# A two-block transformer kernel: SBUF buffers allocated in another order

## What is computed

```
x = first_block(x, ...)    # mod = silu(c) @ w_ada; h = rms_norm(x) * (1 + sc1) + sh1
                           # h @ w_in -> HGRN2, dilated attention, conv module; gates = sigmoid(h @ w_gate)
                           # x += g1 * rms_norm(merged @ w_o)
                           # y = square(relu(h @ w_up)) @ w_down ; x += g2 * rms_norm(y)
return second_block(x, ...)  # the same frame: mLSTM and differential attention with a context of 256
                             # tokens, then (silu(gate) * val) @ w_down with a depthwise conv of 3
```

## Time and profile before

| | |
|---|---|
| median of 3 runs | 3175.56 us (3174.21 to 3181.29) |
| span of the profiled execution | 3166.6 us; its whole time was not recorded, so 9.0 us lie between its span and the median |
| granted TensorE clock, mean | 0.995 of 2.4 GHz |
| PE busy | 98% of the span, 23,974 matmuls |
| PEld busy | 93% |
| DVE, ACT busy | 75%, 42% |
| DMA | 722.62 MB, 228 GB/s over the span |

### The profile page before, as it was taken

How to read it: one execution, slowest core, us unless ns; L and a number is a source line. 1 busy time by engine, 2 the same in 40 slices (tenths; PEclk the granted TensorE clock), 3 DMA queues, 4 the chain that set the end, 5 groups by cost and what they waited for, 6 DMA issues and landing times.

```text
span 3166.6 us, 55394 instructions
## 1 busy us (share of the span) xinstructions
PE 3099.8 (98%) x23974; PEld 2933.4 (93%) x23974; DVE 2369.1 (75%) x2843; ACT 1334.2 (42%) x1459; POOL 1.8 (0%) x10
## 2 busy tenths in 40 slices
PE   7999999999999999999999999999999999999997
PEld 6899999999999999998988999989889989999996
DVE  4799876688887889899978765644767666767766
ACT  3343344444444443333463334422455444344444
POOL 0000000000000000000000000000000000000000
PEclk9999999999999999999999999999999999999999
DMA  9864444498894887777855763354343475655743
GB/s 395 333 216 168 162 158 149 173 352 344 328 366 160 311 306 273 269 264 288 297 186 212 274 256 139 134 217 160 120 147 134 174 265 187 226 213 201 258 177 136
DMA packets 106417, 722.62 MB, mean 228 GB/s; under 512 B 11677, under 2 KB 15389, under 8 KB 27197
## 3 DMA queue, kind: packets, MB, share of 16 engines
q1 hardware_dynamic: 100368, 703.64, 59.6%
q10 hardware_dynamic: 5806, 15.43, 1.6%
HBM read 712.41 MB, written 6.55 MB: 227 GB/s over the span
## 4 chain that ended last, share of the span: by engine, by line
PE 90%; DVE 6%; DMA 1%; ACT 1%; issue 1%; ACTq 0%; DVEq 0%
PE gemm L1040 40%; PE gemm L1049 19%; PE gemm L1076 12%; PE gemm L1079 6%; PE mix L1040 1%; DVE sb_parts L1781 1%; PE mix L1291 1%; PE mix L1571 1%; DMA sb_arena<-x_t 1%; ACT sb_parts L539 1%; DMA sb_raw<-stream 1%; DVE sb_arena L1836 1%; PE gemm L1207 1%; PE mix L1049 1%; PE mix L1150 1%
## 5 line engine op out<-in xcount | busy, mean ns | idle before, releaser
L539 ACT ACTIVATE sb_parts<-sb_raw 128x2048 fp32r<-128x2048 f32 (+2 forms) x489 | 899.6, 1842 | 1464.1 <-PE gemm L1049 958.9
L1781 DVE TENSOR_TENSOR sb_parts<-sb_raw,sb_parts 128x2048 fp32r<-128x2048 f32 (+2 forms) x489 | 1071.9, 2193 | 301.7 <-PE gemm L1049 149.9
L1040 PE MATMUL gemm<-op_h,sb_parts 128*128 128x256 f32 x7232 | 876.5, 278 | 1.1 <-ACT sb_parts L539 0.6
L1040 PEld LDWEIGHTS gemm<-op_h,sb_parts 128*128 128x128 f32 x7232 | 853.2, 188 | 2.5 <-ACT sb_parts L539 1.0
L1049 PE MATMUL gemm<-op_h,sb_parts 128*128 128x256 f32 x3616 | 455.4, 278 | 0.0
L1049 PEld LDWEIGHTS gemm<-op_h,sb_parts 128*128 128x128 f32 x3616 | 434.8, 188 | 0.2 <-DVE sb_parts L1781 0.2
L1076 PE MATMUL gemm<-op_up,sb_parts 128*128 128x512 f32 x1728 | 418.0, 392 | 3.0 <-DVE op_up L2410 3.0
L1076 PEld LDWEIGHTS gemm<-op_up,sb_parts 128*128 128x128 f32 x1728 | 315.3, 188 | 65.4 <-DVE op_up L2410 4.8
L1079 PEld LDWEIGHTS gemm<-op_up,sb_parts 128*128 128x128 f32 x1728 | 218.3, 188 | 10.5
L1762 DVE CUSTOM_DVE_ANT_0 sb_raw<-sb_raw,sb_arena,sb_vec 128x2048 f32<-128x2048 f32 x96 | 224.3, 2348 | 1.1
L1079 PE MATMUL gemm<-op_up,sb_parts 128*128 128x256 f32 x1728 | 220.6, 278 | 0.0
(11 more groups left out here) (360 smaller groups left out, 3340.3 us busy)
## 6 DMA issues: line engine op xcount, KB each, us to landing
sb_raw<-stream SPq DMA_DIRECT2D x597, 1024.0 KB, 5.0
sb_raw<-stream SPq DMA_DIRECT2D x64, 704.0 KB, 4.1
sb_arena<-stream SPq DMA_DIRECT2D x14, 1024.0 KB, 7.9
sb_arena<-stream SPq DMA_DIRECT2D x10, 768.0 KB, 8.2
sb_raw<-stream SPq DMA_DIRECT2D x6, 768.0 KB, 7.2
sb_arena<-c_rows ACTq DMA_DIRECT2D x3, 1024.0 KB, 8.4
bias_rows<-sb_arena ACTq DMA_DIRECT2D x1, 2304.0 KB
sb_arena<-x_t ACTq DMA_DIRECT2D x4, 512.0 KB, 19.1
```

The lines of the kernel that those rows point to most:

```text
L539: act.activation(parts[:, b % 2, 0, 0:kt, :], slot_of(slot)[:, 0:kt, :], ACT.Copy).then_inc(hi_ready, 1)
L1040: ins = pe.matmul(out, l, r, start=(opens and i == 0 and x is xh), stop=False, skip_group_check=True)
L1781: dve.tensor_tensor(parts[:, b % 2, 1, 0:kt, :], slot_of(slot)[:, 0:kt, :], parts[:, b % 2, 0, 0:kt, :].bitcast(F32), ALU.subtract).then_i ...
```

## The change

The order of the allocations. `small` (512 bytes) and `mod1` (384 bytes) come first and fill the space from byte 4,224 to 5,120. The arena follows at 5,120 (5 x 1,024), then `raw` at 153,600 (150 x 1,024), `parts` at 186,368 (182 x 1,024), `ident` at 219,136, `ones` at 219,648, and the rest behind them. Sizes, shapes and the use of every buffer stay as they were, and each engine's instructions are the same in the same order; only addresses in them differ.

```diff
-        raw = sb("raw", [P, SLOTS, KT, P])
-        parts = sb("parts", [P, 2, 2, KT, P], F32R)
-        ident = sb("ident", [P, P])
-        ones = sb("ones", [P, P])
-        vec = sb("vec", [P, NVEC])
-        sel = sb("sel", [P, 8])
-        head_sum = sb("head_sum", [P, 64])
+        small = sb("small", [P, 128])
         mod1 = sb("mod1", [P, 96])
-        mod2 = sb("mod2", [P, 2, 96])
-        lvl_mask = sb("lvl_mask", [P, 8, P], U8)
-        rstd = sb("rstd", [P, 512])
-        small = sb("small", [P, 128])
         ARENA = 37120
...
-        max_rows = rstd[0:8, :]
         opYd = operand("yd", 12288, 2, 8, S)
         opU2 = paired("up2", 12288, UP2)
         arena = sb("arena", [P, ARENA])
+        raw = sb("raw", [P, SLOTS, KT, P])
+        parts = sb("parts", [P, 2, 2, KT, P], F32R)
+        ident = sb("ident", [P, P])
+        ones = sb("ones", [P, P])
+        vec = sb("vec", [P, NVEC])
+        sel = sb("sel", [P, 8])
+        head_sum = sb("head_sum", [P, 64])
+        mod2 = sb("mod2", [P, 2, 96])
+        lvl_mask = sb("lvl_mask", [P, 8, P], U8)
+        rstd = sb("rstd", [P, 512])
+        max_rows = rstd[0:8, :]
```

## The result

The changed kernel takes 3238.43 us (median of 4 runs, 3238.04 to 3239.46), the kernel before 3178.26 us (4 runs, 3174.21 to 3181.29). The ratio is 1.0194 with a 95% interval of 1.0164 to 1.0223: slower by 60 us. The forecast was 3131 us, 1.4% faster, with a range of 3105 to 3217. The 60 us are some twice the distance between the shortest and the longest run of the kernel before that is on record (3166.67 to 3196.79 us).

A forecast was written before the change was run, and what follows sets the result against it. PE was taken to bound the kernel, busy for 98% of the span. Slow stretches -27.9, mixed stretches -12.9, down projections -3.8, other engines and DMA 0, sum -44.6 us: 3175.6 to 3131.0 us, range 3105 to 3217.

The forecast's parts named there:

- The two paces: PE's 256-column matmuls inside blocks: 113.4 ns at the quick pace and 117.8 at the slow one, same code and clock.
- two phases: PE's weight and moving reads hinder each other in SBUF and lock in one of two phases: 6.7 or 11.1 ns per matmul.
- the DMAs' 0: DMA at the start, up to some 130 us: aligning `raw` was taken to gain or lose 0 us.
- I take the first: Of three outcomes for PE, the one chosen: all matmuls at the quick pace, together 44.6 us saved.
- by paces that the trace has: PE's price bounded by observed paces: 44.6 us gained if all quick, 40.4 us lost if all slow.
- The slower rival: At distance 0 weight and moving reads meet, all blocks at the slow pace: 40.4 us lost, 3216 us; chance 25%.
- the quick stretches: Stretches of PE work at the quick pace, 6852 matmuls: 30.1 us lost if all turned slow.
- The stretches with both paces: 131:320, 1895:2200 and 2200:2388, 4401 matmuls: two thirds counted slow and on the path, 12.9 us gain; last third 6.5 us loss.
- That of the slower case: Sign in the chain: 32 matmuls of L1040 in up1_1 taking 3.77 us or more, not 3.63, says slower.
- That of a third state: Sign that PE locks in a third state, making the prediction wrong: a 512-column matmul away from 229 ns.
- Nothing changes: The phases come from PE's own pipeline, so addresses do not enter, or they swap places: 3175 us; chance 30%.
- The cost vanishes: Aligned reads need no extra step: up to 202 us less, taken as 123 us, 3052 us; chance 9%.

The follow-up runs named there:

- runs 13: Separate program with PE alone, moving operand 0 to 512 bytes from the weights: 120.0 ns at 0, 117.8 at 64, 118.7 at 128, 113.3 at 192 bytes.
- run 15: Separate program with PE alone, 16 growing stalls per distance: 113.3 or 117.8 ns at 64 and 192 bytes, 113.3 ns all 16 times at 112.
- Run 16: Changed kernel with the arena and all `op_...` operands 112 bytes past a multiple of 256, `parts` on one: 3152.7 us, ratio 0.9879 to the kernel before.
- 17: Separate program with PE alone, 13 pairs of starts (weights, moving): 113.3 ns for 0,112; 120.0 ns for 64,64 and, in three of four, 144,0.
- runs 7 to 12: Changed kernel with 128, 32, 256, 192 or 96 bytes between `raw` and `parts`; kernel before with 64 bytes ahead of the arena; 128 bytes gave 3229 us.

## Why the prediction was wrong

**Right.** That only PE's pace could change, and that VectorE, ScalarE and the clock would not. The two paces and that they aren't DMA traffic. That the pace of before is one of two phases, and that the relative place of the weights and the moving operand is what the change turns: runs 13 and 15 show it with PE alone. That the two reads meet in SBUF is still argued. That the DMAs' 0 held: the matmul that began at 131.0 us before begins at 131.0 after, and from 30 to 130 us they move 416 GB/s.

The Trainium skill, TensorE: Matmul & The Clock Gate, section Step-by-step: what each phase is for, weighed in the prediction, speaks of two independent read ports. What is measured speaks against reading this as reads that can't hinder each other: one program of PE's alone has 113.3 to 120.0 ns, by addresses only. The further transaction that the Trainium skill (DMA: Bandwidth & Descriptors, section How a descriptor splits into AXI transactions) gives for a start off 256 bytes would have brought an estimated 2 us, if it held for writes; these runs show 0.0.

**The step that failed** is "I take the first" under PE, that all blocks would come to the quick pace since "it needs the least to happen". Its basis was that the quick pace is a state that PE holds for long. But that state belonged to the distance of 64 bytes: at distance 0 neither of the two paces of before exists, and all of it runs at a third one, 120.0 ns. The trace of before had a distance of 64 bytes only, one way or the other, so it could not say in which direction a turn goes, and a state held at one distance is no evidence for another. The sentence that bounded the price "by paces that the trace has" is the same error for the range.

**The slower rival** named the mechanism, two reads that meet at equal remainders, and the place, first the merge stage. What was mis-sized in it is the pace: 117.8 ns taken, 120.0 measured. With it, the quick stretches' 6852 matmuls cost 6.6 ns each, 45.2 us (42.3 measured; the rival had 30.1), and the slow ones, which the rival left alone, 6343 x 2.2 = 14.0 us (13.2 measured). The merge stage alone took 15.7 us and not 10.5. The down projections were taken at 3.8 us and gave 5.6, as their narrow matmuls went to 119.4 ns. The stretches with both paces were taken at 6.5 us and gave 9.7. So the rival's 40.4 us became 70 against the profiled execution, and 60 between the medians. The objection to it, that a weight stream half as dense can't meet the columns all the time at any distance, doesn't bear on the price: the cost at the worst distance is 13.3 ns a matmul beyond its columns, against 11.1 at the slow pace of before.

**Two smaller readings.** The counts of the earlier trace rows were taken as matmuls of 256 columns; some are of 512, 384 of the 1740 from 1895 to 2200 us above all. And in the three stretches with both paces some 85% of the narrow matmuls were slow, where two thirds were counted as slow and on the path. Neither changes the outcome.

**The signs to look for.** That of the slower case was written rightly: up1_1 at 3.77 us or more says slower, and it is at 3.84. That of a third state, a matmul of 512 columns away from 229 ns, was not: the third pace came for 256 columns while the wide ones stayed at 229 (228.9 on average).

**The other rivals.** Nothing changes: refuted, though what it held for it is true as well: in run 15 the pace differs from stall to stall, at one address. The cost vanishes: no placement that was tried brought the narrow matmul's pace below 113.3 ns, so its floor of 106.7 wasn't reached. Run 16 puts more matmuls at the quick pace and takes nothing off that pace.

**What stays open.** Why the steps are a quarter of 256 bytes, what chooses the phase after a stall (its length differed from group to group in run 15, so it may be the length), why placements within 64 bytes aren't told by their distance, and why wide matmuls prefer other distances (229 ns at 0, 192 and 256 in the kernel, 233 and 234 at 32 to 128) than narrow ones. The numbers show the map and not the memory behind it. Only two placements off the 32-byte grid were tried in the whole kernel, one of `parts` and one of the arena; a better one, also for `parts` as the moving operand, wasn't looked for.

## What to carry to other kernels

A PE-bound kernel in which every matmul loads its own weights has a knob that no instruction shows: where the loaded and the moving operand begin relative to each other. Read the distance of the starts over whole stretches; if the same shape at the same clock has more than one pace, or one well above the 113.3 ns for 256 columns that was the least here (6% above the columns), shift one buffer by 64 bytes and measure. Don't take round numbers for safe, since equal remainders gave the slowest pace here. Before a reordering of allocations is judged neutral, compare that distance before and after.

## What the runs showed of the hardware

- For fp32r with 128 loaded columns and 256 moving ones, the pace with PE alone is 120.0 ns when both starts have the same remainder of 256 bytes and are multiples of 64, 118.6 to 118.8 at a distance of 128 bytes, 113.3 or 117.8 at 64 and 192, and always 113.3 with the weights on 0 and the moving operand on 112 (runs 13, 15 and 17). In the three programs together that is 23 groups of 23.
- At 64 and 192 bytes the pace is settled behind a stall (slow to quick 14 to 2 and 5 to 11 in run 15), and in the kernel before PE kept it over 2382 matmuls on end from 586 to 856 us.
- For 512 columns PE alone has 226.7 ns with the moving operand 0 and 256 bytes past the weights and 228.9 at 64, against 233.2 at 192 (runs 13 and 15): an order of its own. It is that of the whole kernel, where the table of runs 7 to 12 counts from the other side (233 at 64, 229 at 192).
- The spread from run to run goes with this: 3166.67 to 3196.79 us at a distance with two paces, 3237.86 to 3241.08 at 256 bytes with one.
